# A two-model transformer kernel: memory attention by heads, with its outputs in rows of features, and six extra products in each up projection

## The reference

```python
def memory_cross_attention(h, mem_n, ...):        # first model, 4 heads of 256
    q, k, v = h @ w_xq, mem_n @ w_xk, mem_n @ w_xv
    s = einsum('bshd,bmhd->bhsm', q, k) * 256 ** -0.5
    p = softmax(s, axis=-1)
    return einsum('bhsm,bmhd->bshd', p, v).reshape(B, S, D_MODEL) @ w_xo

def memory_cross_attention_2(h, mem, ...):        # second model, 4 heads of 128
    q = rms_norm_2(h @ w_mq, q_g)
    k, v = ...                                    # keys normed in the same way
    p = softmax(einsum('bthd,bmhd->bhtm', q, k) * 128 ** -0.5, axis=-1)
    return einsum('bhtm,bmhd->bthd', p, v).reshape(B, T, 512) @ w_mo

hdn = square(relu(rms_norm(x) @ w_up)); x = x + norm(hdn @ w_down)   # after it, in every layer
```

## Time and profile before

| | |
|---|---|
| median of 3 runs | 1355.44 us (1353.64 to 1355.97) |
| the profiled execution | 1356.83 us, of which the span from the first to the last instruction is 1354.9 us |
| TensorE busy | 1302.4 us, 96% of the span |
| VectorE busy | 834.9 us, 62% |
| ScalarE busy | 669.7 us, 49% |
| mean granted TensorE clock | 0.982 |

### The profile page before, as it was taken

The page is one execution under the profiler, slowest core; times in us unless marked ns, Lnnn a source line. Parts: engine busy times, 40 slices in busy tenths (PEclk is TensorE's granted clock), DMA queues, the critical chain, the costliest instruction groups (busy, mean ns, idle before and its releaser), DMA issues.

```text
span 1354.9 us, 23638 instructions
## 1 busy us (share of the span) xinstructions
PE 1302.4 (96%) x10335; PEld 1260.7 (93%) x10335; DVE 834.9 (62%) x919; ACT 669.7 (49%) x948; POOL 87.5 (6%) x65
## 2 busy tenths in 40 slices
PE   3999999999999999999999999999998988999998
PEld 3999999999999999999999999998897887999998
DVE  5478537567654559745657674468658676676542
ACT  4466546455533447545546543345436544465432
POOL 3000010110001100002020000111000100100000
PEclk8999999999999999999999999999698999999999
DMA  5644454246555354444435656555331231366552
GB/s 183 210 132 141 163 175 137 94 125 214 191 187 187 113 156 128 157 139 142 129 121 157 212 166 209 186 142 164 125 104 53 94 115 44 122 208 196 187 187 94
DMA packets 195573, 202.92 MB, mean 150 GB/s; under 512 B 5716, under 2 KB 191847, under 8 KB 195471
## 3 DMA queue, kind: packets, MB, share of 16 engines
q1 hardware_dynamic: 192704, 194.82, 45.0%
q0 software_dynamic: 2464, 5.99, 1.5%
q10 hardware_dynamic: 303, 0.61, 0.2%
HBM read 200.33 MB, written 3.16 MB: 150 GB/s over the span
## 4 chain that ended last, share of the span: by engine, by line
PE 85%; DVE 6%; ACT 4%; DMA 2%; issue 2%; POOL 1%; DVEq 0%; ACTq 0%; POOLq 0%
PE bank L560 14%; PE bank L562 14%; PE bank L561 14%; PE bank L2219 7%; PE bank L2215 7%; PE bank L2217 7%; PE bank L603 3%; PE bank L611 2%; PE bank L605 2%; DVE w_lo L524 2%; PE bank L2035 2%; PE bank L2132 2%; ACT w_hi L514 2%; PE bank L2116 1%; PE bank L2062 1%
## 5 line engine op out<-in xcount | busy, mean ns | idle before, releaser
L524 DVE TENSOR_TENSOR w_lo<-raw,w_hi 128x2048 fp32r<-128x2048 f32 (+7 forms) x210 | 424.1, 2029 | 344.6 <-ACT w_hi L514 344.2
L514 ACT ACTIVATE w_hi<-raw 128x2048 fp32r<-128x2048 f32 (+7 forms) x210 | 354.9, 1702 | 374.9 <-PE bank L2219 138.7
L560 PE MATMUL bank<-act_hi,w_hi 128*128 128x256 f32 x1096 | 310.1, 283 | 0.0
L562 PE MATMUL bank<-act_hi,w_lo 128*128 128x256 f32 x1096 | 307.4, 280 | 0.0
L561 PE MATMUL bank<-act_lo,w_hi 128*128 128x256 f32 x1096 | 307.4, 280 | 0.0
L2215 PE MATMUL bank<-h_hi,w_hi 128*128 128x256 f32 x768 | 215.4, 280 | 0.0
L2217 PE MATMUL bank<-h_lo,w_hi 128*128 128x256 f32 x768 | 215.2, 280 | 0.0
L2219 PE MATMUL bank<-h_hi,w_lo 128*128 128x256 f32 x768 | 215.2, 280 | 0.0
L561 PEld LDWEIGHTS bank<-act_lo,w_hi 128*128 128x128 f32 x1096 | 208.4, 190 | 0.2
L562 PEld LDWEIGHTS bank<-act_hi,w_lo 128*128 128x128 f32 x1096 | 206.9, 189 | 0.0
L560 PEld LDWEIGHTS bank<-act_hi,w_hi 128*128 128x128 f32 x1096 | 206.2, 188 | 0.8 <-issue 0.3
(11 more groups left out here) (354 smaller groups left out, 2172.3 us busy)
## 6 DMA issues: line engine op xcount, KB each, us to landing
raw<-in_w_up_dram SPq DMA_DIRECT2D x32, 1024.0 KB, 5.4
raw<-in_w_down_dram SPq DMA_DIRECT2D x32, 1024.0 KB, 5.1
raw<-in_w_ff_dram SPq DMA_DIRECT2D x32, 1024.0 KB, 5.4
raw<-in_w_in_dram SPq DMA_DIRECT2D x23, 1024.0 KB, 5.2
raw<-in_w_xk_dram SPq DMA_DIRECT2D x8, 1024.0 KB, 5.1
raw<-in_w_xv_dram SPq DMA_DIRECT2D x8, 1024.0 KB, 5.2
raw<-in_w_mix_out_dram SPq DMA_DIRECT2D x8, 1024.0 KB, 5.1
raw<-in_w_xq_dram SPq DMA_DIRECT2D x8, 1024.0 KB, 5.2
```

The source lines that it names most:

```text
L514: ins = act.activation(d, r, ACT.Copy)
L524: ins = dve.tensor_tensor(d, r, h.bitcast(F32), ALU.subtract)
L560: pe.matmul(o, stat_hi, mov_hi, start=first, stop=False)
L562: return pe.matmul(o, stat_lo, mov_hi, start=False, stop=last)
```

## The change

In the memory attention of both models a unit becomes one head with all 256 tokens. The probabilities are divided by the row sums before they are transposed (`divided`), the transposed blocks are laid out so that both halves of the tokens lie side by side, and the values become the stationary operand. The product with the values then has features in rows and tokens in columns, which is what the output projection reads. ScalarE and VectorE split it in two parts straight from the bank (`head_part`, `head_rest`). `o_out`, the transpositions `ot` 4 to 7 (4 and 5 in the second model) and their `o_part` and `o_rest` go. The scores of a head wait for the queries of that head alone (in the second model of that half). In `TE_ORDER`, the first half of slab 28 now stands before `pv` 14 and 15. The two `keep_clock` products before `ot` 4 of the second model go.

Apart from that, in each of the three up projections six products of the fifth slab with itself are formed ahead of that slab's own products, in the bank that these then overwrite (`weights_first`).

```diff
-     ("pv", 12), ("pv", 13), ("turn", 14), ("turn", 15), ("ot", 4), ("ot", 5), ("pv", 14), ("pv", 15),
-     ("half", 28), ("ot", 6), ("ot", 7), ("half", 29), ("rest", 28), ("rest", 29), ("slab", 30), ("slab", 31),
+     ("pv", 12), ("pv", 13), ("turn", 14), ("turn", 15),
+     ("half", 28), ("pv", 14), ("pv", 15), ("half", 29), ("rest", 28), ("rest", 29), ("slab", 30), ("slab", 31),
...
-          ("scores", 12): ("scores12", 14), ("ot", 4): ("ot4", 2), ("slab", 25): ("mo0", 2)}
+          ("scores", 12): ("scores12", 14), ("slab", 25): ("mo0", 2)}
...
-     ("turn", 15), ("pv", 14), ("pv", 15)] + [("ot", 4), ("ot", 5)]
+     ("turn", 15), ("pv", 14), ("pv", 15)]
...
+            def head_part(layer, b, tile0, used):
+                act.wait_ge(sig["pv"], value("pv", layer, used))
+                act.activation(o_hi[:, tile0:tile0 + 2, :], halves(bank(f"o{b}", layer)[:, :]), ACT.Copy)\
+                    .then_inc(sig["o_hi"], 1)
...
+                head_part(layer, 4, 0, 13)
+                head_part(layer, 5, 2, 14)
+                turned_out(layer, 15)
                 load_table(ACT.Sqrt)
-                o_part(layer, 4, 0, 0)
-                turned_out(layer, 15)
-                o_part(layer, 5, 0, 1)
-                o_part(layer, 6, 4, 0)
-                o_part(layer, 7, 4, 1)
+                head_part(layer, 6, 4, 15)
+                head_part(layer, 7, 6, 16)
...
             for b in range(4, 6):
-                o_part(DEPTH, b, 0, b - 4)
+                head_part(DEPTH, b, 2 * (b - 4), 14 + 2 * (b - 4))
...
+            def divided(layer, u):
+                c = 32 + 2 * (u - 12)
+                dve.wait_ge(sig["probs"], value("probs", layer, u + 1))
+                dve.reciprocal(row_inv[:, c:c + 2], row_sum[:, c:c + 2]).then_inc(sig["rinv"], 1)
+                dve.wait_ge(sig["rinv"], value("rinv", layer, u - 7))
+                p = halves(probs[:, u % P_RING, :])
+                dve.tensor_tensor(p, p, row_inv[:, c:c + 2].unsqueeze(2).broadcast_to([P, 2, T]), ALU.mult)\
+                    .then_inc(sig["p_scaled"], 1)
+
+            def head_rest(layer, b, tile0):
+                dve.wait_ge(sig["o_hi"], value("o_hi", layer, b + 1))
+                dve.tensor_tensor(o_lo[:, tile0:tile0 + 2, :], halves(bank(f"o{b}", layer)[:, :]),
+                                  o_hi[:, tile0:tile0 + 2, :].bitcast(F32), ALU.subtract).then_inc(sig["o_lo"], 1)
...
                 x_max(13)
                 split_lo(dve, layer, 29)
+                divided(layer, 12)
+                divided(layer, 13)
                 x_query(3)
                 turned_out(layer, 12)
                 x_max(14)
                 x_max(15)
-                o_out(layer, 4, 12, 32, 2)
-                o_out(layer, 5, 13, 34, 2)
+                divided(layer, 14)
+                divided(layer, 15)
+                head_rest(layer, 4, 0)
+                head_rest(layer, 5, 2)
                 turned_out(layer, 14)
                 split_lo(dve, layer, 30)
-                o_rest(layer, 4, 0, 0)
-                o_rest(layer, 5, 0, 1)
-                o_out(layer, 6, 14, 36, 2)
-                o_out(layer, 7, 15, 38, 2)
-                o_rest(layer, 6, 4, 0)
-                o_rest(layer, 7, 4, 1)
+                head_rest(layer, 6, 4)
+                head_rest(layer, 7, 6)
...
                 dve.tensor_reduce(neg_max[:, c:c + 2], halves(bank(f"scores{u}", DEPTH)[:, :]), AX.X, ALU.max,
                                   negate=True).then_inc(sig["neg_max"], 1)
+                if u > 12:
+                    divided(DEPTH, u - 1)
             turned_out(DEPTH, 12)
+            divided(DEPTH, 15)
             split_lo(dve, DEPTH, 26)
             turned_out(DEPTH, 14)
             split_lo(dve, DEPTH, 27)
-            dve.wait_ge(once["b_sum"], 4)
-            for i in range(TI):
-                o_out(DEPTH, 4 + i, 13 + 2 * i, 32 + 4 * i, 4)
-            for i in range(TI):
-                o_rest(DEPTH, 4 + i, 0, i)
+            for n in range(2):
+                head_rest(DEPTH, 4 + n, 2 * n)
...
+            def weights_first(layer, s, use):
+                b = open_bank(pe, layer, use)
+                pe.wait_ge(sig["slab_lo"], value("slab_lo", layer, s + 1))
+                w = w_hi[:, slot(layer, s)]
+                for k in range(6):
+                    pe.matmul(b[:, 0:T], w[:, T * k:T * k + P], w[:, T * k:T * k + T], start=True, stop=True)
...
-                    i, heads = x_unit(u - 12)
-                    pe.wait_ge(sig["z_evac"], value("z_evac", layer, 18 + heads[0]))
-                    for n, h in enumerate(heads):
+                    h = u - 12
+                    pe.wait_ge(sig["z_evac"], value("z_evac", layer, 17 + h))
+                    for i in range(TI):
...
-                pe.wait_ge(sig["probs"], value("probs", layer, u + 1))
+                if u < 12:
+                    pe.wait_ge(sig["probs"], value("probs", layer, u + 1))
+                else:
+                    pe.wait_ge(sig["p_scaled"], value("p_scaled", layer, u - 11))
...
-                            ins = pe.matmul(b[:, T * m:T * m + T], pt[:, P * (2 * m + c):P * (2 * m + c) + P],
-                                            vx[:, c, T * h:T * h + T], start=c == 0, stop=c == 1)
+                            ins = pe.matmul(b[:, T * m:T * m + T], vx[:, c, T * h + P * m:T * h + P * m + P],
+                                            pt[:, T * c:T * c + T], start=c == 0, stop=c == 1)
...
+                    if (kind, n) == ("slab", 36):
+                        weights_first(layer, 36, "up4")
                     steps[kind](layer, n)
...
-                    pe.wait_ge(once["hs_done"], 8)
+                    h = u - 12
+                    pe.wait_ge(once["hs_done"], 7 + h // 2)
...
+                    for c in range(TI):
+                        ins = pe.matmul(b[:, T * (h % 2):T * (h % 2) + T], mem_v[:, c, P * h:P * h + P],
+                                        pt[:, T * c:T * c + T], start=c == 0, stop=c == 1)
...
+                if (kind, n) == ("slab", 31):
+                    weights_first(DEPTH, 31, "up4")
                 steps_2[kind](n)
```

More of the change, by code:

```diff
@@ L102 @@
 PER = {
-    "slab_used": 64, "stat_mm": 7, "kpe_mm": 1, "scores": 16, "p_turned": 16, "pv": 16, "o_turned": 8,
+    "slab_used": 64, "stat_mm": 7, "kpe_mm": 1, "scores": 16, "p_turned": 16, "pv": 16, "o_turned": 4,
     "first_bank": 5,
@@ L112 @@
     "slab_lo": 64, "act_lo": 32, "rstd": 4, "back_inv": 3, "x_back": 8, "both_roots": 1, "gains": 1, "g_next": 1, "rope_k": 1, "z_evac": 20, "c_norm": 2,
-    "c_lo": 5, "biased": 12, "neg_max": 16, "pt_v": 8, "o_evac": 8, "rinv": 8, "o_lo": 8,
+    "c_lo": 5, "biased": 12, "neg_max": 16, "pt_v": 8, "o_evac": 4, "rinv": 8, "p_scaled": 4, "o_lo": 8,
     "x_part": 24, "x_new": 24, "up_scaled": 16, "h_lo": 16,
@@ L208, in bank_uses_2 @@
             if opens:
-                uses.append((f"o{b}", "o_evac", b + 1))
+                uses.append((f"o{b}", "o_evac" if b < 4 else "o_lo", b + 1))
         elif kind == "cpv":
@@ L288, in bank_uses @@
         elif o_bank(n)[1]:
-            uses.append((f"o{o_bank(n)[0]}", "o_evac", o_bank(n)[0] + 1))
+            uses.append((f"o{o_bank(n)[0]}", "o_evac" if n < 12 else "o_lo", o_bank(n)[0] + 1))
     return uses + [None] * (-len(uses) % N_BANKS)
@@ L655, in unit_2 @@
             return 1, range(2 * u - 4, 2 * u - 2), 2
[L657 to L661, removed]
         branch_root = root[:, T + TI:2 * T + TI]
@@ L2113, in turn @@
                 b = open_bank(pe, layer, f"turn{u}")
-                pe.wait_ge(sig["probs"], value("probs", layer, u + 1))
+                if u < 12:
+                    pe.wait_ge(sig["probs"], value("probs", layer, u + 1))
+                else:
+                    pe.wait_ge(sig["p_scaled"], value("p_scaled", layer, u - 11))
                 for n in range(4):
-                    ins = pe.transpose(b[:, P * n:P * n + P], probs[:, u % P_RING, P * n:P * n + P], ident)
+                    to = n if u < 12 else 2 * (n % 2) + n // 2
+                    ins = pe.transpose(b[:, P * to:P * to + P], probs[:, u % P_RING, P * n:P * n + P], ident)
                 ins.then_inc(sig["p_turned"], 1)
@@ L2134, in pv @@
                 else:
-                    i, heads = x_unit(u - 12)
-                    for m, h in enumerate(heads):
+                    h = u - 12
+                    for m in range(2):
                         for c in range(TI):
-                            ins = pe.matmul(b[:, T * m:T * m + T], pt[:, P * (2 * m + c):P * (2 * m + c) + P],
-                                            vx[:, c, T * h:T * h + T], start=c == 0, stop=c == 1)
+                            ins = pe.matmul(b[:, T * m:T * m + T], vx[:, c, T * h + P * m:T * h + P * m + P],
+                                            pt[:, T * c:T * c + T], start=c == 0, stop=c == 1)
                 ins.then_inc(sig["pv"], 1)
@@ L2345, in scores_2 @@
```

(34 more changed lines are left out.)

2 lines of the change are left out of this document (1 added, 1 removed).

## The result

Over six runs each the changed kernel took 1342.62 us in the median (1336.78 to 1346.01), the kernel before 1355.7 (1350.16 to 1357.02). The ratio is 0.9901, with a 95% interval from 0.9883 to 0.992: 1.0% faster, some 13 us, where 0.5 us was forecast. In a later set of runs (e12) the same kernel gave 0.9877 (0.9848 to 0.9907) and a median of 1339.15 us. Executions of one kernel differ by some 10 us, and the longer ones tend to have the lower mean granted clock (of the changed kernel's six, the longest, 1346.01 us, had 0.974 and the shortest, 1336.78, had 0.984).

A forecast was written before the change was run, and what follows sets the result against it. TensorE, busy for 1302.4 of 1354.9 us, was taken as the bound. The terms −1.1 − 0.4 − 1.2 + 2.2 = −0.5 us took the median from 1355.44 to 1354.9 us; range 1352.6 to 1358.0.

The forecast's parts named there:

- the six products: Three up projections: 18 added products at 0.12 us each, with no cover, cost +2.16 us.
- lower end of zero: Added products in the up projections: they cost nothing if a wait the trace does not show stands behind them.
- First layer, −1.1: First layer's memory attention: 16 transpositions go, divisions before `turn` are hidden; −1.1 us.
- Second layer, −0.4 between −1.1 and +0.3: Second layer's attention: loses 0.3 us if slab 28's load is late, else wins 1.1; mean taken, −0.4.
- Second model, −1.2: Second model's attention: VectorE's queue from first maximum, 12.85 us without rest, lets slab 25 start 1.2 us earlier.
- The clock: Slower rival, second model's attention: granted clock falls in emptier stretches; sum +1.2 to +2.9 us; chance 0.14.
- the faster rival: Extra products cost nothing (−3.4 us, 1352.1), or a low-clock stretch costing 1.7 us goes; chance 0.14, dropped products included.
- Divisions late in both layers: Slower rival, first model's attention: TensorE waits for divisions in both layers; sum +1.6 us, 1357.0; chance 0.12.
- The products were not dropped: Rival on the up projections' added products: the compiler drops them; sum −2.7 us, 1352.8; chance 0.01.
- the forecast of −2.7: Whole kernel: the sum in us if the compiler dropped the added products, leaving the attention's terms; 1352.8 us.

The follow-up runs named there:

- e12: The changed kernel again, unedited, in a later set of runs; 0.9877, 1339.15 us.
- e3: Changed kernel, but its six added products are of the ordinary kind (weights stand still, activations move); 1.0008, 1356.01 us.
- e2: Changed kernel without the six added products, so the new attention alone; 0.9975, 1351.5 us.
- e4: Changed kernel with one added product in each place instead of six; 0.9939, 1347.79 us.
- e10: Changed kernel with three added products instead of six, in seven kinds of places, among them before each up projection's first whole slab; 0.9853, 1336.15 us.

## Why the prediction was wrong

**The step that failed** is the one on the six products: "They are dense short-format work between slabs where TensorE does not wait, so I see no cover. Ends: nothing, … 18 × 0.28 = 5.0 …" I took one step of 0.12 us for every product of the kernel, and so counted only the 18 that came in. Six products of the ordinary kind cost that, as e3 shows: +0.71 in each stretch. But the step of the other products is no constant. With the changed kernel's operands the six put the 1338 that follow from 117.8 to 113.3 ns: −6.0 us in a layer, +0.7 for themselves, −5.3 in sum, and −5.23 measured. The term forecast at +2.16 was −14.0. Its lower end of zero excluded any gain, and I had given no reason why there could be none.

**The trace of before held the clue.** Stretches of 5 us of it, each full of products at a granted clock of 1.00: slab 19, which has the weights as the moving operand, and slabs 20 to 23 behind it, with activations moving again; first layer, then second:

```profile
174.00:179.00 5.00, 5.00 (x45) 5.00 (x44) 3.49 (x3) 2.20 (x3) 0.00 (x0) 1.00 0.16 40
180.00:185.00 5.00, 5.00 (x47) 5.00 (x46) 2.29 (x1) 1.90 (x2) 0.00 (x0) 1.00 0.40 142
...
603.00:608.00 5.00, 5.00 (x44) 5.00 (x44) 3.41 (x3) 2.53 (x3) 0.00 (x0) 1.00 0.16 55
610.00:615.00 5.00, 5.00 (x47) 5.00 (x46) 2.29 (x1) 1.90 (x2) 0.00 (x0) 1.00 0.34 113
```

45 and 44 products, then 47 and 47: both rates, and the change from the one to the other within a microsecond of the point where products with a moving weight end. In all fourteen profiles slabs 20 to 23 of both layers run at 113.3 ns. The view that would have shown it is the count of products in equal stretches, over the whole span; I read single steps, in the attention, where nearly all were slow.

**First layer, −1.1: right.** 1.41 us won up to the first half of slab 29 (1.31 in e2). Some 0.2 of it was not forecast: the first half of slab 28 took 2.83 us (242.30 to 245.13) where it had taken 3.02, in part by the faster rate. `turn` 12 has no wait, and the first half of slab 28 waits 0.54 for VectorE's rest where 0.7 was forecast.

**Second layer, −0.4 between −1.1 and +0.3: the mechanism right, the end too near.** The load of slab 28 was later still (5.34 us of ScalarE's waiting, 4.63), the division came 1.69 late, and the window lost 0.84. In e2 it won 0.42. Taking the mean of the two layers was the weak point: in all twelve profiles with the new attention the second layer waits for the division (0.30 to 1.69 us) and the first never does, so the first layer's win was no likely end for the second. The wait tends to be longer where ScalarE waits longer for slab 28's load (0.41 us at 3.87 in e2, 1.23 at 4.89 in e4, 1.69 at 5.34 here).

**Second model, −1.2: right in kind, 0.9 measured.** VectorE is the bound: its chain took 13.1 us where 12.85 was summed, and slab 25 starts 0.1 after its end. In e2 the window won only 0.2.

**The rivals.** The clock did not fall in the second model's attention, although the stretches got as empty as foreseen; in the changed kernel's stretches of 5 us (columns as above) 3.15 and 3.28 us busy stand beside a granted clock of 1.00:

```profile
1130.00:1135.00 5.00, 3.15 (x16) 2.08 (x15) 4.44 (x9) 2.95 (x12) 0.00 (x0) 1.00 0.00 0
1135.00:1140.00 5.00, 3.28 (x20) 2.52 (x18) 4.93 (x8) 1.86 (x6) 0.00 (x0) 1.00 0.00 0
```

The stretch at the low clock that the faster rival named did go, but another came, in the second layer, where the kernel before has 1.00. Changed kernel:

```profile
1105.00:1110.00 5.00, 5.00 (x46) 5.00 (x46) 4.21 (x9) 4.15 (x7) 1.29 (x1) 1.00 0.55 202
470.00:475.00 5.00, 5.00 (x35) 5.00 (x35) 3.60 (x5) 2.08 (x6) 0.00 (x0) 0.75 0.73 216
```

The stretch behind it has 0.91. Together they are as much at half speed as the stretch at 0.66 was, so the two cancel. Divisions late in both layers did not come in these executions, only in the second. The products were not dropped (line 2057, x6). The rival on the faster side had them cost nothing; that they could give something was in no case, so the range ended at 1352.6. Without the six products the forecast of −2.7 agrees with e2's ratio, −3.4 (−1.6 to −5.1).

## What to carry to other kernels

Where TensorE is the bound, count its products in equal stretches over the whole span before taking any step between two of them as a price: two counts at one granted clock mean that the stream has another rate, which may be won. Here a few products with the weights as the moving operand, put right ahead of a long run of products with moving activations, were worth 14 us of 1355, their own 2 us paid; with three in each place at the first whole slab, some 16. An instruction whose result nobody reads can still change what comes after it, so its lower bound isn't zero until a row says so.

## What the runs showed of the hardware that was not expected

- A dense stream of weight load and 128 x 256 product has two lasting rates, 113.3 and 117.8 ns from start to start, at a granted clock of 1.00 (its 2.4 GHz level). A rate once taken held for up to 1440 products. The Trainium skill ("TensorE: Matmul & The Clock Gate", section on the back-to-back issue gap) says that in such a stream the spacing is set by both the weight load and the matmul; it gives one spacing for a size, where these traces have two for the same instructions.
- Among the weight loads, the recorded time of one differs with the rate: that of the second product of each three, which loads the block that stands already. Groups by line of TensorE's weight loads, 300 to 450 us, before:

```profile
L2217 PEld LDWEIGHTS bank<-h_lo,w_hi 128*128 128x128 f32 x232 | 44.5, 192 | 0.0
L2215 PEld LDWEIGHTS bank<-h_hi,w_hi 128*128 128x128 f32 x232 | 43.5, 188 | 0.0
```

and in the changed kernel:

```profile
L2241 PEld LDWEIGHTS bank<-h_hi,w_hi 128*128 128x128 f32 x252 | 47.3, 188 | 0.0
...
L2243 PEld LDWEIGHTS bank<-h_lo,w_hi 128*128 128x128 f32 x251 | 47.1, 188 | 0.0
```

  At the slow rate that load takes 192 ns and at the fast one 188; the load of the block's first use takes 188 in both. That the stream is slow because of it is not shown.
- The fast rate is also taken where no weight moves just ahead, and not each time. Behind fillers and a wait, the 96 products that run around 210 us in the first layer (slabs 24 and 25) ran at 113.3 ns in eight of the fourteen profiles and at 117.8 in six, with the same instructions ahead of them in all but e10. The kernel before and the changed one:

```profile
206.50:214.50 8.00, 8.00 (x73) 8.00 (x72) 7.53 (x17) 5.47 (x12) 2.08 (x2) 1.00 0.01 2
206.50:214.50 8.00, 8.00 (x71) 8.00 (x70) 6.52 (x15) 5.56 (x10) 3.08 (x2) 1.00 0.01 2
```

  So moving weights are one way to that rate. In the three long stretches, which begin behind float32 sums, it was the only one seen.
- The output transpositions near the end change the rate too, in either direction and not each time. In the kernel before, the slabs behind the first of them ran at 113.3 ns after a slow stretch. In the changed kernel the rate stays fast over the first and falls to 117.8 at the second: 170 products in 19 us ahead of that, 163 behind.

```profile
1290.00:1309.00 19.00, 19.00 (x170) 19.00 (x169) 9.28 (x5) 6.63 (x5) 0.00 (x0) 1.00 0.59 199
1312.00:1331.00 19.00, 19.00 (x163) 19.00 (x163) 5.19 (x3) 3.01 (x3) 0.00 (x0) 1.00 0.21 70
```

  There the changed kernel loses some 0.9 us to the kernel before (191 products of 4.5 ns).
- Not settled: what the two rates are, why a moving weight leads to the fast one, and why one or three products, or six with an activation standing, do it only in some places.
